# Strassen's seven products for every second weight chunk in the first three down halves of a two-block float32 kernel

## Chip, cores and metric

The kernel runs on one core of one Trainium2 chip. The metric is the device time of one execution in microseconds (us), lower is better. Times "before" are those of the kernel as it stood; the change is then made to it and nothing else.

## The reference

Two blocks work on 256 tokens of width 2048, all in float32. The first is a mixer (a gated linear recurrence beside a banded attention) followed by an MLP; the second is an attention block with 16 meta tokens. The change touches the MLP of the first block alone:

```python
u = rms_norm(h, norm_mlp_w[l])
h = h + jnp.square(jax.nn.relu(u @ w_up[l])) @ w_down[l]    # w_up 2048 x 8192, w_down 8192 x 2048
```

## The kernel before

**Weights as a stream of chunks.** Every weight matrix of the program goes through one ring. A chunk is 256 rows by 512 columns of a weight (two tiles of 128 rows, CK = 2, by CW = 512 columns, 512 KB), and eight chunks (NC) are a group: 2048 rows by 512 columns. The ring has four slots (SLOTS). For each chunk SyncE's queue issues one load into `raw` (`chunk`, line 366) as soon as the lower half of the chunk four places earlier is done (`wlo_ready`). Then the float32 values are split in two parts of which TensorE can multiply each in one pass: ScalarE copies `raw` to `whi` with rounding (`split_hi`, line 887), and it waits for the load and for TensorE being done with the chunk four places earlier (`pe_done`). VectorE subtracts, `wlo = raw - whi` (`split_lo`, line 1301). TensorE waits for `wlo_ready` of the chunk and multiplies three times for each product: high by high, high by low and low by high. ScalarE and VectorE work four chunks ahead of TensorE (LEAD = 4): in their loops, step `k` of a group splits chunk `k + 4`.

**The MLP** is cut into four quarters of 2048 hidden columns (`quarter`: line 682 for TensorE, 1100 for ScalarE, 1588 for VectorE, 1970 for GpSimd). A quarter has two halves of four groups each. In the up half `chunk_t` (line 430) makes four hidden blocks of 128 columns by 256 tokens for each group in PSUM: ScalarE takes the relu, GpSimd squares it (`relu2`), ScalarE copies the square to the high part in `ya_hi` or `yb_hi`, VectorE subtracts for the low part. These are the activations of the down half. There `chunk_n` (line 451) sets tokens stationary and streams weights: for each of two row tiles, two token tiles and two pieces of 256 columns it issues three matmuls, so 2 x 2 x 2 x 3 = 24 matmuls of 256 columns for each chunk. After a group VectorE adds the sum, times a factor for each token, to `h` (`scalar_tensor_tensor`, line 1617). Up and down groups take banks 0 to 3 of PSUM by turns (`set_free`).

**Order on the engines.** Each engine works its list in order. On VectorE and ScalarE the splits are the backbone, and the rest of a group stands behind the splits of the group. GpSimd has nothing but the squares in these quarters, 16 in all.

**The names that the change brings.** In a chunk, A is the 256 tokens by 256 rows of activations and B the 256 rows by 512 columns of weights. Cut in 2 by 2 blocks their product takes eight block products, each 128 tokens by 128 rows by 256 columns; Strassen's scheme (in Winograd's form) takes seven, with sums of blocks on both sides.

Of the kernel before, what the change touches and what calls it, by code (L numbers as in the profile page):

```python
# [60 lines left out]
C_END = C_OUT2 + 4 * NC  # L61

# [49 lines left out]
def program(nc, x, w_in, lb_logits, hg_norm_w, rel_bias, w_branch_a, w_branch_b, w_out, norm_mix_w,  # L112
# [3 lines left out]
    with ExitStack() as ctx:  # L116
# [100 lines left out]
        relu2 = at("relu2", 96, [P, 4, T])  # L217
        fin_w = at("fin_w", 80, [P, D])
# [66 lines left out]
        br_m, br_hi, br_ready = sem("br_m"), sem("br_hi"), sem("br_ready")  # L285
        up_sq, up_hi, up_ready = [sem(n) for n in ("up_sq", "up_hi", "up_ready")]
# [40 lines left out]
        def kv_banks(j):  # L327

            return (0, 4) if j % 2 == 0 else (2, 6)

# [96 lines left out]
        def _(pe):  # L427
# [23 lines left out]
            def chunk_n(c0, k, kt0, xh, xl, s, first, last, halves=range(NT), pieces=1):  # L451

                pe.wait_ge(wlo_ready, c0 + k + 1)
                for j in range(CK):
                    kt = kt0 + j
                    for t in halves:
                        toks = slice(t * P, (t + 1) * P)
                        for piece in range(pieces):
                            cols = slice(piece * CW // pieces, (piece + 1) * CW // pieces)
                            for i, (v, w) in enumerate(((xh, whi), (xh, wlo), (xl, whi))):  # L460
                                ins = mm(ps[:, 2 * s + t, cols], v[:, kt, toks], w[:, k % SLOTS, j, cols],  # L461
                                         start=first and j == 0 and i == 0 and piece == 0,
                                         stop=last and j == CK - 1 and i == 2, skip_group_check=True)
# [218 lines left out]
            def quarter(q, first=False, last=False):  # L682

                c0 = C_FF + 8 * NC * q
                for g in range(4):
                    pe.wait_ge(set_free[g % 2], G_IN // 2 + 6 + 4 * q + g // 2)
                    for k in range(NC):
# [4 lines left out]
                        chunk_t(c0 + NC * g, k, CK * k, x2hi, x2lo, blocks(g % 2), T, k == 0, k == NC - 1)  # L692
                for g in range(4):
                    pe.wait_ge(set_free[g % 2], G_IN // 2 + 8 + 4 * q + g // 2)
                    for k in range(NC):
                        pe.wait_ge(up_ready, 4 * q + k // 2 + 1)
                        uh, ul = (ya_hi, ya_lo) if k < NC // 2 else (yb_hi, yb_lo)
# [3 lines left out]
                        chunk_n(c0 + 4 * NC + NC * g, k, CK * (k % (NC // 2)), uh, ul, g % 2, k == 0, k == NC - 1,  # L701
# [182 lines left out]
        def _(act):  # L884
            f = nc.scalar.activation

            def split_hi(c0, k):
# [4 lines left out]
                f(whi[:, k % SLOTS], raw[:, k % SLOTS], ACT.Copy).then_inc(whi_ready, 1)  # L892

# [206 lines left out]
            def quarter(q, first=False, last=False):  # L1100
                c0 = C_FF + 8 * NC * q
                for g in range(4):
                    for k in range(NC):
                        split_hi(c0 + NC * g, LEAD + k)
# [8 lines left out]
                    f(relu[:], pset(g % 2), ACT.Relu).then_inc(set_free[g % 2], 1)  # L1113
# [3 lines left out]
                for g in range(4):  # L1117
                    for k in range(NC):
                        split_hi(c0 + 4 * NC + NC * g, LEAD + k)
                        if last and g >= 1:  # L1120
# [7 lines left out]
                            if k == 4:  # L1128
                                scaled_squares(g - 1)

# [160 lines left out]
        def _(dve):  # L1291
# [9 lines left out]
            def split_lo(c0, k):  # L1301

                dve.wait_ge(whi_ready, c0 + k + 1)
                tt(wlo[:, k % SLOTS], raw[:, k % SLOTS], whi[:, k % SLOTS], ALU.subtract).then_inc(wlo_ready, 1)  # L1304

# [282 lines left out]
            def quarter(q, first=False, last=False):  # L1588
                c0 = C_FF + 8 * NC * q
                for g in range(4):  # L1590
                    for k in range(NC):
                        split_lo(c0 + NC * g, LEAD + k)
# [14 lines left out]
                for g in range(4):  # L1607
                    for k in range(NC):
                        split_lo(c0 + 4 * NC + NC * g, LEAD + k)
                        if last and g >= 1 and k == 1:  # L1610
                            wide_lower(g - 1)
                        if last and g == 1 and k == 5:
                            nc.vector.tensor_copy(xw_lo[:, :, T:TM], mlo).then_inc(m_lo_placed, 1)
                    dve.wait_ge(pe_done, c0 + 4 * NC + NC * (g + 1))
# [249 lines left out]
        def _(pool):  # L1864
# [192 lines left out]
```

## Time and profile before

| | |
|---|---|
| time, median of 3 runs | 1884.91 us (1884.53 to 1887.14) |
| the profiled execution | 1885.47 us, of which the span from first to last instruction is 1883.7 us |
| TensorE busy | 1870.7 us (99%), 15001 matmuls recorded |
| VectorE, ScalarE busy | 1101.3 us (58%), 890.0 us (47%) |
| GpSimd busy | 149.8 us (8%), 133 instructions |
| granted TensorE clock, mean | 0.999 |
| HBM | 183 GB/s over the span |

The quarters of the MLP lie from about 725 to 1428 us of the span. "Busy" is the time in which an engine had an instruction under way; the durations of single matmuls overlap, so the pace of TensorE is read from a stretch of many of them and not from the mean of one. A line of the trace ends with the idle time of the engine just before the instruction and what ended it. L1304 is VectorE's split of the weights, L892 ScalarE's, L447 and L461 are the matmuls of `chunk_t` and `chunk_n`, and L371 the loads.

### The profile page before, as it was taken

Reading aid. Unit: us, or ns where it says so; the run is one execution under the profiler, and the core shown is the slowest. Engines: PE = TensorE matmul, PEld = TensorE weight load, DVE = VectorE, ACT = ScalarE, POOL = GpSimd, SP = SyncE. Lnnn points to the kernel's source line nnn. Section 1 sums busy time; section 2 is a strip of 40 time slices with the busy share of each in tenths; the row PEclk is TensorE's granted clock in tenths of the full one; section 3 lists DMA queues with packets and bytes.
Section 4 is the critical chain, followed back from the end, with each engine's and each line's share of the span. In section 5 each row is a group of like instructions: output and inputs, shape, how many; then the busy total and the mean of one; then the engine's idle time right before and its main releaser. Section 6 shows DMA issues by size and latency. Waiting matters only on the chain.

```text
span 1883.7 us, 37025 instructions
## 1 busy us (share of the span) xinstructions
PE 1870.7 (99%) x15001; PEld 1802.9 (96%) x15001; DVE 1101.3 (58%) x1270; ACT 890.0 (47%) x1171; POOL 149.8 (8%) x133
## 2 busy tenths in 40 slices
PE   9999999999999999999999999999999999999998
PEld 9989998999999989999999999999989999899998
DVE  6645766667655555545445545544566556867664
ACT  6544443465544445443444344334554345574543
POOL 1001322411001100000000000001010000000000
PEclk9999999999999999999999999999999999999999
DMA  8666566566665666666666666666656665355464
GB/s 270 191 178 176 182 179 179 163 197 180 177 223 192 214 186 185 185 203 195 196 192 194 197 188 197 197 192 193 193 184 179 177 175 159 113 168 146 157 191 145
DMA packets 176927, 347.94 MB, mean 185 GB/s; under 512 B 11152, under 2 KB 11360, under 8 KB 176256
## 3 DMA queue, kind: packets, MB, share of 16 engines
q1 hardware_dynamic: 174176, 337.76, 58.8%
q0 software_dynamic: 2608, 8.08, 1.7%
q8 instruction: 114, 1.87, 0.4%
q14 instruction: 29, 0.24, 0.0%
HBM read 342.37 MB, written 2.10 MB: 183 GB/s over the span
## 4 chain that ended last, share of the span: by engine, by line
PE 98%; DVE 1%; ACT 0%; DMA 0%; issue 0%; SPq 0%; DVEq 0%; ACTq 0%
PE ps L447 60%; PE ps L461 32%; PE ps L551 1%; PE ps L784 1%; PE ps L774 1%; PE ps L794 1%; PE ps L751 0%; PE ps L479 0%; PE ps L762 0%; PE ps L602 0%; PE ps L594 0%; PE ps L492 0%; DMA x_nat<-in_x_dram 0%; PE ps L613 0%; PE ps L735 0%; ACT whi L892 0%
## 5 line engine op out<-in xcount | busy, mean ns | idle before, releaser
L1304 DVE TENSOR_TENSOR wlo<-raw,whi 128x1024 fp32r<-128x1024 f32 x631 | 796.6, 1269 | 688.2 <-ACT whi L892 687.3
L892 ACT ACTIVATE whi<-raw 128x1024 fp32r<-128x1024 f32 x631 | 664.9, 1059 | 883.2 <-PE ps L447 549.8
L447 PE MATMUL ps<-xhi,whi 128*128 128x256 f32 (+1 forms) x1904 | 541.5, 284 | 0.3 <-DVE qrot L1667 0.3
L447 PE MATMUL ps<-xhi,wlo 128*128 128x256 f32 (+1 forms) x1904 | 531.3, 279 | 0.0
L447 PE MATMUL ps<-xlo,whi 128*128 128x256 f32 x1664 | 462.5, 278 | 0.0
L447 PEld LDWEIGHTS ps<-xhi,whi 128*128 128x128 f32 x1904 | 359.3, 189 | 8.8 <-issue 6.2
L447 PEld LDWEIGHTS ps<-xhi,wlo 128*128 128x128 f32 x1904 | 357.9, 188 | 0.0
L447 PEld LDWEIGHTS ps<-xlo,whi 128*128 128x128 f32 x1664 | 313.2, 188 | 1.2 <-issue 0.5
L447 PE MATMUL ps<-x2hi,whi 128*128 128x256 f32 x1024 | 282.8, 276 | 0.0
L447 PE MATMUL ps<-x2lo,whi 128*128 128x256 f32 x1024 | 282.7, 276 | 0.0
L447 PE MATMUL ps<-x2hi,wlo 128*128 128x256 f32 x1024 | 282.7, 276 | 0.0
L447 PEld LDWEIGHTS ps<-x2lo,whi 128*128 128x128 f32 x1024 | 192.2, 188 | 0.2
L447 PEld LDWEIGHTS ps<-x2hi,whi 128*128 128x128 f32 x1024 | 192.2, 188 | 0.2
L447 PEld LDWEIGHTS ps<-x2hi,wlo 128*128 128x128 f32 x1024 | 192.2, 188 | 0.0
L461 PE MATMUL ps<-whi,ya_hi 128*128 128x256 f32 (+1 forms) x464 | 133.8, 288 | 0.0
L461 PE MATMUL ps<-whi,ya_lo 128*128 128x256 f32 (+1 forms) x464 | 133.7, 288 | 0.0
L461 PE MATMUL ps<-wlo,ya_hi 128*128 128x256 f32 (+1 forms) x464 | 133.6, 288 | 0.0
L461 PE MATMUL ps<-whi,yb_lo 128*128 128x256 f32 (+1 forms) x452 | 131.8, 292 | 0.0
L461 PE MATMUL ps<-whi,yb_hi 128*128 128x256 f32 (+1 forms) x452 | 131.7, 291 | 0.0
L461 PE MATMUL ps<-wlo,yb_hi 128*128 128x256 f32 (+1 forms) x452 | 131.6, 291 | 0.0
L461 PE MATMUL ps<-whi,xlo 128*128 128x512 f32 x256 | 100.8, 394 | 0.0
L461 PE MATMUL ps<-whi,xhi 128*128 128x512 f32 x256 | 100.2, 391 | 0.0
(371 smaller groups left out, 2727.3 us busy)
## 6 DMA issues: line engine op xcount, KB each, us to landing
raw<-in_w_in_dram SPq DMA_DIRECT2D x279, 512.0 KB, 3.8
raw<-in_w_up_dram SPq DMA_DIRECT2D x128, 512.0 KB, 3.8
raw<-in_w_down_dram SPq DMA_DIRECT2D x128, 512.0 KB, 4.0
raw<-in_w_out_dram SPq DMA_DIRECT2D x64, 512.0 KB, 4.4
raw<-in_w_branch_a_dram SPq DMA_DIRECT2D x16, 512.0 KB, 5.2
raw<-in_w_branch_b_dram SPq DMA_DIRECT2D x16, 512.0 KB, 4.6
x_nat<-in_x_dram SPq DMA_DIRECT2D x4, 512.0 KB, 7.1
rel<-in_rel_turned_dram POOLq DMA_DIRECT2D x8, 256.0 KB, 4.4
```

The source lines that it names most:

```text
L447: ins = mm(outs[b], w[:, k % SLOTS, j, cols], v, start=start, stop=last and j == CK - 1 and i == 2, skip_group_check=True)
L461: ins = mm(ps[:, 2 * s + t, cols], v[:, kt, toks], w[:, k % SLOTS, j, cols], start=first and j == 0 and i == 0 and piece == 0, stop=last a ...
L551: ins = mm(misc[:, hd // 4, (hd % 4) * P:(hd % 4 + 1) * P], k_both[:, hd, :], spread(qp[:, hd, 0:1], *both_tiles), start=True, stop=True)
L774: ins = nc.tensor.transpose(ps[:, 6, i * P:(i + 1) * P], p[:, i * P:(i + 1) * P], ident[:])
L784: ins = mm(ps[:, 7, 0:P], pt2[:, u % 2, i * P:(i + 1) * P], v, start=i == 0, stop=i == 2)
L794: ins = mm(ps[:, 7, 0:T], v, pt_heads[hd % 2][:, i, :], start=i == 0, stop=i == 2)
L892: f(whi[:, k % SLOTS], raw[:, k % SLOTS], ACT.Copy).then_inc(whi_ready, 1)
L1304: tt(wlo[:, k % SLOTS], raw[:, k % SLOTS], whi[:, k % SLOTS], ALU.subtract).then_inc(wlo_ready, 1)
```

## The change

In quarters 0 to 2 (`SEVEN_Q = 3`), every even chunk of a down group is multiplied by `chunk_seven`; the odd chunks and the last quarter stay with `chunk_n`. That makes 3 quarters x 4 groups x 4 = 48 chunks with 7 x 3 = 21 matmuls in the place of 24.

- **TensorE**: seven products into partial sums of 256 columns, numbered 0 to 7, in four banks; the odd chunks add to partials 0 to 3, which are the output's own blocks. Up groups now use banks 4-5, 6-7, 0-1, 2-3, down groups by turns banks 4-7 and 0-3.
- **GpSimd**: for each such chunk `weight_sums`, one instruction of 128x512 and two of 128x256 in float32, each of which waits for the one before. For each up group, behind the square, `token_sums`: four instructions of 128x128. The three weight sums of down group 0, chunks 0, 2 and 4, stand ahead of the square of up group 3.
- **ScalarE and VectorE**: in such a chunk three quarters of `raw` are split as before (128x768), and then the four weight sums (128x1024, `t_hi` and `t_lo`). VectorE signals `wlo_ready` at the end of `t_lo`, and the slot is loaded anew only then. Token sums are split once for each up group (128x512).
- **The end of a down group**: ScalarE copies one partial to SBUF (`c_first`, 128x256), VectorE adds partials from PSUM to `c_sum` by four additions of 128x512, two of them in step 0, one and one more in step 1 of the next group (behind its splits), and step 2 adds `c_sum`, scaled, to `h` by two instructions of 128x512.

```diff
+SEVEN_Q = QUARTERS - 1
+SEVEN_EACH = NC // 2
+UP_SETS = (2, 3, 0, 1)
...
+            def chunk_seven(c0, k, b, first, last):
+                pe.wait_ge(wlo_ready, c0 + k + 1)
...
+                parts = ((0, sums(3), weights(1, 0)), (1, given(odd, 0), weights(1, 1)),
+                         (3, given(odd, 1), weight_sums(3)), (4, given(even, 0), weights(0, 1)),
+                         (5, sums(1), weight_sums(1)), (6, sums(2), weight_sums(2)), (7, sums(0), weight_sums(0)))
+                for n, (vh, vl), (wh, wl) in parts:
+                    for i, (v, w) in enumerate(((vh, wh), (vh, wl), (vl, wh))):
+                        ins = mm(ps[:, b + n // 2, (n % 2) * T:(n % 2) * T + T], v, w,
+                                 start=first and i == 0 and n in (0, 3, 4, 6), stop=last and i == 2,
+                                 skip_group_check=True)
+                ins.then_inc(pe_done, 1)
...
                         pe.wait_ge(up_ready, 4 * q + k // 2 + 1)
+                        if seven(q, k):
+                            pe.wait_ge(s_ready, 4 * q + k // 2 + 1)
+                            chunk_seven(c0 + 4 * NC + NC * g, k, down_banks(g), k == 0, k == NC - 2)
+                            continue
...
+            def split_hi_seven(c0, k, n):
+                act.wait_ge(raw_in[k % SLOTS], 4 * c0 + 16 * (k // SLOTS + 1))
+                act.wait_ge(pe_done, c0 + k - SLOTS + 1)
+                f(whi[:, k % SLOTS].rearrange("p j c -> p (j c)")[:, T:4 * T],
+                  raw[:, k % SLOTS].rearrange("p j c -> p (j c)")[:, T:4 * T], ACT.Copy).then_inc(whi_ready, 1)
+                act.wait_ge(t_summed, n + 1)
+                f(t_hi[:, k // 2 % 2], t_sum[:, k // 2 % 2], ACT.Copy).then_inc(t_upper, 1)
...
+                    if not last:
+                        act.wait_ge(pe_done, c0 + 4 * NC + NC * (g + 1))
+                        f(c_first[:], ps[:, down_banks(g) + 2, 0:T], ACT.Copy).then_inc(c_copied, 1)
...
+            def split_lo_seven(c0, k, n):
+                dve.wait_ge(whi_ready, c0 + k + 1)
+                part = [v[:, k % SLOTS].rearrange("p j c -> p (j c)")[:, T:4 * T] for v in (wlo, raw, whi)]
+                tt(*part, ALU.subtract)
+                dve.wait_ge(t_upper, n + 1)
+                tt(t_lo[:, k // 2 % 2], t_sum[:, k // 2 % 2], t_hi[:, k // 2 % 2], ALU.subtract).then_inc(wlo_ready, 1)
...
+            def seven_out(q, g, step):
+                b, n = down_banks(g), 16 * q + 4 * g
+                if step == 0:
+                    dve.wait_ge(pe_done, C_FF + 8 * NC * q + 4 * NC + NC * (g + 1))
+                    dve.wait_ge(c_copied, 4 * q + g + 1)
+                    tt(summed(1, 4), spread(c_first[:, 0:1], [0, 2], [1, T]), partial(b, 1, 6), ALU.add).then_inc(c_step, 1)
+                    dve.wait_ge(c_step, n + 1)
+                    tt(summed(5, 6), summed(4), partial(b, 5, 7), ALU.add).then_inc(c_step, 1)
...
+                        if g >= 1 and k < 3 and not last:
+                            seven_out(q, g - 1, k)
...
+            def weight_sums(q, g, k):
+                c0, n = C_FF + 8 * NC * q + 4 * NC + NC * g, seven_at(q, g, k)
+                w, to = raw[:, k % SLOTS], t_sum[:, k // 2 % 2]
+                pool.wait_ge(raw_in[k % SLOTS], 4 * c0 + 16 * (k // SLOTS + 1))
+                pool.wait_ge(wlo_ready, c0 + k - SLOTS + 1)
+                tt(to[:, 0:2, :], spread(w[:, 0, 0:1], [0, 2], [1, T]), spread(w[:, 0, T:T + 1], [T, 2], [1, T]),
+                   ALU.subtract).then_inc(t_step, 1)
+                pool.wait_ge(t_step, 2 * n + 1)
+                tt(to[:, 2, :], w[:, 1, 0:T], to[:, 0, :], ALU.subtract).then_inc(t_step, 1)
+                pool.wait_ge(t_step, 2 * n + 2)
+                tt(to[:, 3, :], w[:, 1, T:2 * T], to[:, 2, :], ALU.subtract).then_inc(t_summed, 1)
...
-            with pool.Fori(0, QUARTERS) as q:
+            with pool.Fori(0, SEVEN_Q) as q:
                 for g in range(4):
-                    pool.wait_ge(set_free[g % 2], G_IN // 2 + 6 + 4 * q + g // 2 + 1)
-                    tt(relu2[:], relu[:], relu[:], ALU.mult).then_inc(up_sq, 1)
+                    if g == 3:
+                        for k in range(0, 6, 2):
+                            weight_sums(q, 0, k)
+                    squared(q, g)
+                    token_sums(q, g)
+                for g in range(4):
+                    for k in range(0, NC, 2):
+                        if g > 0 or k == 6:
+                            weight_sums(q, g, k)
+            for g in range(4):
+                squared(SEVEN_Q, g)
```

## Rows read from the trace of the kernel before

**Rows 1.** The chain that ended last, from 725 us: start, us, what.

```profile
732.02 81.62 PE ps L447 x720
813.64 87.07 PE ps L461 x756
```

**Rows 2.** Busy time by engine in an up half and the down half behind it.

```profile
core 0: us, PE busy (x) PEld busy (x) DVE busy (x) ACT busy (x) POOL busy (x), PEclk, DMA share, GB/s
725.40:812.50 87.10, 87.10 (x770) 87.05 (x769) 44.52 (x43) 43.49 (x48) 6.12 (x3) 1.00 0.64 190
812.50:899.70 87.20, 87.20 (x764) 86.88 (x763) 44.38 (x40) 35.73 (x34) 2.02 (x1) 1.00 0.64 195
```

**Rows 3.** The same columns in the first 6 us.

```profile
0.00:6.00 6.00, 2.79 (x12) 2.38 (x12) 0.40 (x3) 1.49 (x2) 4.22 (x12) 1.00 0.50 155
```

**Rows 4.** Timeline from up group 3 to down group 0: start, us, instruction, idle before it.

```profile
813.74 1.06 ACT L892 ACTIVATE whi<-raw 128x1024 fp32r<-128x1024 f32 x1 [1.66 <-PE ps L447]
...
817.84 1.06 ACT L1116 ACTIVATE yb_hi<-relu 128x1024 fp32r<-128x1024 f32 x1 [2.13 <-POOL relu L1973]
...
815.79 2.02 POOL L1973 TENSOR_TENSOR relu<-relu 128x1024 f32<-128x1024 f32 x1 [19.74 <-ACT relu L1113]
...
814.83 1.23 DVE L1304 TENSOR_TENSOR wlo<-raw,whi 128x1024 fp32r<-128x1024 f32 x1 [1.50 <-ACT whi L892]
818.93 1.23 DVE L1606 TENSOR_TENSOR yb_lo<-relu,yb_hi 128x1024 fp32r<-128x1024 f32 x1 [2.88 <-ACT yb_hi L1116]
820.08 2.35 DVE L1304 TENSOR_TENSOR wlo<-raw,whi 128x1024 fp32r<-128x1024 f32 x2
```

**Rows 5.** GpSimd's groups by form: count, busy us, mean ns, idle before.

```profile
L1973 POOL TENSOR_TENSOR relu<-relu 128x1024 f32<-128x1024 f32 x16 | 32.4, 2025 | 663.3 <-ACT relu L1113 663.3
L1894 POOL TENSOR_TENSOR pairs<-pairs,masked 128x512 f32<-128x512 f32 x12 | 15.5, 1295 | 107.9 <-DVE masked L1463 107.9
L1967 POOL TENSOR_TENSOR both<-part_a,part_b 128x1024 f32<-128x1024 f32 x4 | 9.6, 2400 | 141.6 <-DVE part_b L1570 141.6
```

**Rows 6.** Timeline of VectorE and GpSimd where the last quarter scales h.

```profile
1387.18 2.42 POOL L1979 TENSOR_TENSOR h<-h,fin_w 128x1024 f32<-128x1024 f32 x1 [20.43 <-PE ps L479]
...
1387.35 3.33 DVE L1304 TENSOR_TENSOR wlo<-raw,whi 128x1024 fp32r<-128x1024 f32 x1 [1.52 <-ACT whi L892]
```

**Rows 7.** Timeline of both where the recurrence adds its tiles.

```profile
335.56 2.41 POOL L1899 TENSOR_TENSOR acc<-acc,masked 128x1024 f32<-128x1024 f32 x1 [21.97 <-DVE masked L1469]
340.27 3.31 POOL L1899 TENSOR_TENSOR acc<-acc,pairs 128x1024 f32<-128x1024 f32 x1 [2.30 <-DVE pairs L1469]
...
335.87 3.18 DVE L1304 TENSOR_TENSOR wlo<-raw,whi 128x1024 fp32r<-128x1024 f32 x1 [0.39 <-ACT whi L892]
338.97 1.21 DVE L1469 TENSOR_TENSOR pairs<-pairs,tri 128x1024 f32<-128x1024 f32 x1
340.11 5.69 DVE L1304 TENSOR_TENSOR wlo<-raw,whi 128x1024 fp32r<-128x1024 f32 x3
```

**Rows 8.** Timeline of both at one level of the recurrence.

```profile
238.06 1.29 POOL L1894 TENSOR_TENSOR pairs<-pairs,masked 128x512 f32<-128x512 f32 x1 [1.76 <-DVE masked L1463]
239.31 1.39 POOL L1912 TENSOR_TENSOR g_even<-g_odd 128x128 f32<-128x128 f32 x1
...
238.54 1.90 DVE L1304 TENSOR_TENSOR wlo<-raw,whi 128x1024 fp32r<-128x1024 f32 x1 [0.56 <-ACT whi L892]
```

**Rows 9.** VectorE's groups by form.

```profile
L1304 DVE TENSOR_TENSOR wlo<-raw,whi 128x1024 fp32r<-128x1024 f32 x631 | 796.6, 1269 | 688.2 <-ACT whi L892 687.3
L1617 DVE SCALAR_TENSOR_TENSOR h<-ps,rstd,h 128x512 f32<-128x512 f32 x32 | 22.4, 743 | 0.0
L1463 DVE TENSOR_TENSOR masked<-ps,masks 128x512 f32<-128x512 f32 x12 | 8.2, 680 | 0.0
L1493 DVE TENSOR_TENSOR o_hg<-o_hg,rs_hg 128x512 f32<-128x512 f32 x4 | 2.7, 684 | 0.0
```

**Rows 10.** Loads of the down weights: count, KB each, us from issue to landing.

```profile
raw<-in_w_down_dram SPq DMA_DIRECT2D x128, 512.0 KB, 4.0
```

More of the change, by code:

```diff
@@ L217, in program @@
         relu2 = at("relu2", 96, [P, 4, T])
+        s_sum = at("s_sum", 92, [P, 4, P])
+        t_sum = at("t_sum", 100, [P, 2, 4, T])
+        c_sum = at("c_sum", 108, [P, 8, T])
+        c_first = at("c_first", 94, [P, T])
+        s_hi, s_lo = [v[:, 0:4 * 4 * P].rearrange("p (g i t) -> p g i t", g=4, i=4) for v in x_flat]
+        t_hi, t_lo = [v[:, 4 * 4 * P:KT * T].rearrange("p (n i c) -> p n i c", n=2, i=4) for v in x_flat]
         fin_w = at("fin_w", 80, [P, D])
@@ L466, in chunk_n, with given, sums, weights @@
                 return ins
+            def chunk_seven(c0, k, b, first, last):
+                pe.wait_ge(wlo_ready, c0 + k + 1)
+                uh, ul = (ya_hi, ya_lo) if k < NC // 2 else (yb_hi, yb_lo)
+                even, odd = CK * k % (NC), CK * k % (NC) + 1
+                toks = slice(0, P), slice(P, T)
+                slot, turn = k % SLOTS, k // 2 % 2
+                def given(kt, t):
+                    return uh[:, kt, toks[t]], ul[:, kt, toks[t]]
+                def sums(i):
+                    return s_hi[:, k // 2, i, :], s_lo[:, k // 2, i, :]
+                def weights(j, half):
+                    cols = slice(half * T, half * T + T)
+                    return whi[:, slot, j, cols], wlo[:, slot, j, cols]
+                def weight_sums(i):
+                    return t_hi[:, turn, i, :], t_lo[:, turn, i, :]
+                parts = ((0, sums(3), weights(1, 0)), (1, given(odd, 0), weights(1, 1)),
[7 more added lines that the diff above has]
+                ins.then_inc(pe_done, 1)
             def blocks(s):
@@ L700, in quarter @@
                         whole = last and g >= 1 or g == 3 and k == NC - 1
[L701 removed]
+                        chunk_n(c0 + 4 * NC + NC * g, k, CK * (k % (NC // 2)), uh, ul,
+                                g % 2 if last else down_banks(g) // 2, k == 0, k == NC - 1,
                                 pieces=1 if whole else 2)
@@ L1613, in quarter @@
                             nc.vector.tensor_copy(xw_lo[:, :, T:TM], mlo).then_inc(m_lo_placed, 1)
+                    if not last:
+                        if g == 3:
+                            for step in range(3):
+                                seven_out(q, g, step)
+                        continue
                     dve.wait_ge(pe_done, c0 + 4 * NC + NC * (g + 1))
@@ new lines, in token_sums @@
+            def token_sums(q, g):
+                first, second = [[relu2[:, i, t * P:(t + 1) * P] for i in range(2)] for t in range(NT)]
+                pool.wait_ge(up_sq, 4 * q + g + 1)
+                tt(s_sum[:, 1, :], second[0], first[0], ALU.subtract).then_inc(s_step, 1)
+                tt(s_sum[:, 0, :], second[0], second[1], ALU.add)
+                pool.wait_ge(s_step, 2 * (4 * q + g) + 1)
+                tt(s_sum[:, 2, :], s_sum[:, 1, :], second[1], ALU.add).then_inc(s_step, 1)
+                pool.wait_ge(s_step, 2 * (4 * q + g) + 2)
+                tt(s_sum[:, 3, :], first[1], s_sum[:, 2, :], ALU.subtract).then_inc(s_summed, 1)
```

70 lines of the change are left out of this document (64 added, 6 removed).

## The prediction

> **What bounds the kernel now.** I read first the chain that ended last. In the MLP it is TensorE alone: an up half is one piece of `chunk_t` matmuls, the down half behind it one piece of `chunk_n` matmuls, 87.07 us for its 32 chunks [rows 1]. So a chunk takes 87.07 / 32 = 2.721 us and a matmul of 256 columns 2.721 / 24 = 0.1134 us. Next the busy times by stage: in a down half TensorE is busy for 87.2 of 87.2 us, VectorE for 44.4, ScalarE for 35.7, GpSimd for 2.0 [rows 2]. Last the timeline: a split comes when TensorE is done with the chunk four places before (ScalarE at 813.74, VectorE done at 816.06), while three chunks, 3 x 2.721 = 8.2 us, still lie ahead of TensorE. The lead is 8.2 - 2.3 = 5.8 us [rows 4]. The chip is bound by the count of matmuls, and anything that shortens the list pays, as long as VectorE keeps ahead.
>
> **What is removed.** 3 of 24 matmuls in 48 chunks: 16 x 3 x 0.1134 = 5.44 us for each down half, 16.3 us in all. An even chunk takes 2.381 us, a pair 5.10.
>
> **What is added on GpSimd.** The reader should look at what two engines do to each other. GpSimd scaled `h` from 1387.18 to 1389.60, and a split that VectorE began at 1387.35 took 3.33 us in the place of 1.23 [rows 4, 6]: it ended at 1390.68, which is 1389.45 + 1.23. So it stood still until 0.15 us short of GpSimd's end. The same at 335.87: 3.18 us, end 339.05 = 337.82 + 1.23, with GpSimd's end at 337.97 [rows 7]. At 340.27 it is the other way: VectorE was first (340.11), GpSimd's addition took 3.31 us and not 2.41, about the 1.0 us that VectorE's first split still had, and VectorE's other two then waited (three in 5.69 us, where two back to back take 2.35 [rows 4, 7]). And the 1.39 us of a GpSimd instruction of only 128x128 at 239.31 is mostly waiting for VectorE's split that ended at 240.44 [rows 8]. Two instructions that both read two tensors of SBUF take turns, whole ones.
>
> The three weight sums read two SBUF tensors each. 128x512 takes 1.30 us, 128x1024 2.40 [rows 5]; the line through both gives 0.74 us for 128x256 and 0.47 for 128x128. The other end for 128x256 is the 1.39 us of rows 8; I take 0.74, since the additions of rows 5 are the nearest in kind and the 1.39 is explained. Less the 0.14 us at the end in which VectorE already runs, a chunk's sums close the way for 1.16 + 0.60 + 0.60 = 2.36 us. [...]
>
> **What is added on VectorE.** For a pair of chunks: 128x768 of the even chunk, between 0.68 us for 128x512 and 1.22 for 128x1024 [rows 4, 9], so 0.95; the sums' lower half and the odd chunk 1.17 each, back to back [rows 4]. For a group's end: four additions of 128x512 from PSUM at 0.68 and two of 0.74 [rows 9], 4.2 us where 1.5 stood.
>
> **The sum for one quarter.** Take the 32 steps from the split of down chunk 0 (TensorE done with chunk 4 of up group 3) to that of the last down chunk. TensorE would want that last one after three up chunks and 31 down chunks: 3 x 2.721 + 16 x 2.381 + 15 x 2.721 = 87.1 us. In this stretch VectorE has 16 x 3.29 = 52.6, three group ends 12.6, the lower half of the last squares 1.2 and of the last token sums 0.7: 67.1 us. Alone it would fit. GpSimd closes the way for 15 x 2.36 = 35.4 (the first chunk's sums run before the stretch), for the square 1.9 and for four token sums 4 x 0.33 = 1.3: 38.6 us. Together 105.7. To this come 2 us in which VectorE waits for ScalarE (today it stands idle 2.88 us ahead of the last squares' lower half [rows 4]; most of that is now GpSimd's). From it goes what runs side by side: VectorE's additions from PSUM read one SBUF tensor, 3 x 2.7 = 8.2 us in the stretch; no row shows one under GpSimd, so between 0 and 8.2 could overlap, and I take half. 105.7 + 2 - 4.1 = 103.6 us, 16.5 more than TensorE wants; the lead of 5.8 us is already in the 87.1. Less 5.44 gained: +11.1 for each quarter, +33 us for three. The profiled execution would go from 1885.47 (span 1883.7) to 1918.7; the median of the runs before is 0.6 lower, so **1918 us**.
>
> The Trainium skill (SBUF — State Buffer, "two separate sides") calls the pair of ports that VectorE and GpSimd share an exclusive lock for a whole instruction, which only VectorE's instructions with two SBUF inputs (or in a two-port mode) ask for. By that rule all 8.2 us would overlap, and the sum would be 1906. The first half of it is what rows 6 and 7 show; the second no row here shows.
>
> **The rest costs nothing, as long as its cover is there.** ScalarE's copies grow from 1.06 us to at most 2 x 1.06 in an even chunk, 16 x 1.06 = 17 us on 35.7 of 87 [rows 2]. The copy `c_first` waits for TensorE's end of a group, but stands behind splits that are four chunks ahead. The loads keep their size, but a slot is free only after the sums' lower half; this matters in rival B. The weight sums for down chunk 4 stand ahead of the square of up group 3; they push that square back by some 2 us, and the squares are wanted only at chunk 6 of the down half, 16 us on. The banks are freed later by `c_sum`, and the next use is a group away. In the up halves VectorE has over 40 us idle [rows 2] for token sums.
>
> **Rivals.**
> A, **the gain comes whole: 1869 us** (1885.5 - 16.3, less 0.6). VectorE's 67.1 us fit in 87.1, if GpSimd's sums fall into its idle time. For: today the two hardly meet. Against: together they have 105.7 us for 87.1. It decides the other way if the turns cost under (87.1 + 5.4 - 67.1 - 2 + 4.1) / 38.6 = 71% of GpSimd's time; rows 6 and 7 show over 90%.
> B, **the round of a slot bounds, 1945 us.** From the end of an even chunk's split to that of the same slot's next: load 4.0 us [rows 10], sums 2.8, each of the three behind one of VectorE's instructions, up to 3 x 1.17, ScalarE's copy 1.06, VectorE's 1.23 behind 1.3 of the other slot's sums: 13.9 us for four chunks, 111 for 32, 24 over 87.1, so +19 net for each quarter, +57 to 60. With half of the waits it is 12 and lies under my 103.6. For: six places to wait in one row. Against: VectorE can't be first at every one.
> C, **TensorE's clock falls** in the waits that now cut up its work, from 2.4 to 1.2 GHz. Matmuls of the down halves would take up to twice as long, over 2000 us. Against: in the first 6 us of the program TensorE had matmuls under way for 2.79 us only and was granted 1.00 [rows 3]; the new waits are under 2 us each.
> D, the costs and the gain meet at about 1885: turns of some 71%.
>
> **How the numbers follow.** Forecast 0.61 (1900 to 1935: all of the PSUM additions under cover and no idle, 105.7 - 8.2 = 97.5, +15 us; none under cover and 4 us idle, 109.7, +51 at the far end); B 0.20; A 0.12; D 0.04; C 0.03. About 0.2% is what a measurement of this kernel tells from no change. Faster 0.12, same 0.03, slower 0.85. The range leaves out A, D, C and the far end of B: 1894 to 1955; the 1.39 us for 128x256 would add 32 x 0.65 = 21 us for each quarter and is left out too, since it is waiting that is counted already. Most cases have one sign, so one range is enough.
>
> **What would show it.** In the down halves of quarters 0 to 2: TensorE idle before the matmuls of `chunk_seven`, released by VectorE's `t_lo`; VectorE busy for more than 90% of such a half, with splits of 1.9 to 2.5 us wherever GpSimd runs; GpSimd about 55 to 60 us busy, its instructions of 128x256 at 0.74 us alone and near 2 behind VectorE; a half of some 98 us where 87.1 stood; 0.1134 us a matmul as before; up halves and the last quarter unchanged. Splits at 1.23 us beside a busy GpSimd would make the forecast wrong and A right; VectorE idle for a fifth of the half, ahead of `t_lo` and released by ScalarE, would make it B.

## Result: 2.0% slower, and the profile after

The changed kernel takes **1922.2 us** (median of 4, 1921.56 to 1924.0) against 1885.01, a ratio of 1.0196 with the 95% interval 1.0184 to 1.0208. The forecast was 1918, with a range of 1894 to 1955. The profiled execution took 1921.56 us. Its page, the span and the engines' busy times:

```profile
span 1919.8 us, 37397 instructions
PE 1875.8 (98%) x14857; PEld 1802.7 (94%) x14857; DVE 1249.7 (65%) x1378; ACT 931.4 (49%) x1243; POOL 391.6 (20%) x325
```

TensorE has fewer matmuls and is busy for longer than before: its matmuls ran slower (experiment 1). VectorE is up by 148 us and GpSimd by 242. The stages of quarter 0, a down half and the up half behind it, with the columns of [rows 2]:

```profile
core 0: us, PE busy (x) PEld busy (x) DVE busy (x) ACT busy (x) POOL busy (x), PEclk, DMA share, GB/s
813.15:912.90 99.75, 87.97 (x710) 85.42 (x709) 86.01 (x68) 46.99 (x53) 65.97 (x47) 1.00 0.53 165
913.00:1000.00 87.00, 87.00 (x769) 87.00 (x768) 50.37 (x46) 41.49 (x43) 21.55 (x21) 1.00 0.61 196
```

The down half takes 99.75 us where 87.07 stood [rows 1], the up half is unchanged. VectorE is busy for 86 of the 99.75 us and not for 44. The span is 36.1 us longer, 12.0 for each down half. TensorE's waits for the sums and for the plain chunks behind them, over the whole program (us in all, times, the longest):

```profile
PE ps L528 <- DVE xlo L1410: 24.1, 18, 3.3
PE ps L495 <- DVE wlo L1402: 5.2, 6, 1.8
```

So it waits for the lower half of the sums, as the prediction said (`t_hi` and `t_lo` lie in the buffers xhi and xlo and are named so; L1410 writes `t_lo`). The groups of GpSimd's sums over the program and of VectorE's splits in the down half show the price of each (count, busy us, mean ns, then idle before):

```profile
L2143 POOL TENSOR_TENSOR t_sum<-raw 128x512 f32<-128x512 f32 x48 | 78.1, 1627 | 83.8 <-DMA raw<-in_w_down_dram 83.8
L2146 POOL TENSOR_TENSOR t_sum<-raw,t_sum 128x256 f32<-128x256 f32 x48 | 73.1, 1523 | 3.8
L2148 POOL TENSOR_TENSOR t_sum<-raw,t_sum 128x256 f32<-128x256 f32 x48 | 60.1, 1251 | 3.8
```

```profile
L1402 DVE TENSOR_TENSOR wlo<-raw,whi 128x1024 fp32r<-128x1024 f32 x16 | 27.2, 1707 | 0.0
L1410 DVE TENSOR_TENSOR xlo<-t_sum,xhi 128x1024 fp32r<-128x1024 f32 x15 | 24.7, 1644 | 8.8 <-ACT xhi L971 8.8
L1408 DVE TENSOR_TENSOR wlo<-raw,whi 128x768 fp32r<-128x768 f32 x15 | 19.5, 1299 | 0.0
L1435 DVE SCALAR_TENSOR_TENSOR h<-c_sum,rstd,h 128x512 f32<-128x512 f32 x6 | 6.1, 1062 | 0.0
```

A 128x256 instruction of GpSimd, 0.74 us alone, takes 1.25 to 1.52 in the mean; a 128x768 part of a split 1.30 where 0.95 was assumed, a full split 1.71 where 1.23 stood [rows 4], an addition to `h` 1.06 for 0.74 [rows 9]. They take turns, and the timeline shows single ones, GpSimd's lines and VectorE's:

```profile
850.00 1.59 POOL L2146 TENSOR_TENSOR t_sum<-raw,t_sum 128x256 f32<-128x256 f32 x1
851.67 0.74 POOL L2148 TENSOR_TENSOR t_sum<-raw,t_sum 128x256 f32<-128x256 f32 x1
...
850.92 0.67 DVE L1423 TENSOR_TENSOR c_sum<-c_first,ps 128x512 f32<-128x512 f32 x1
...
862.36 2.18 POOL L2143 TENSOR_TENSOR t_sum<-raw 128x512 f32<-128x512 f32 x1 [2.69 <-DMA raw<-in_w_down_dram]
864.62 1.61 POOL L2146 TENSOR_TENSOR t_sum<-raw,t_sum 128x256 f32<-128x256 f32 x1
...
862.15 1.21 DVE L1410 TENSOR_TENSOR xlo<-t_sum,xhi 128x1024 fp32r<-128x1024 f32 x1
863.28 2.33 DVE L1402 TENSOR_TENSOR wlo<-raw,whi 128x1024 fp32r<-128x1024 f32 x1
```

GpSimd's 128x512 was issued at 862.36 and waited for VectorE's `t_lo`, which ended at 863.36; then VectorE's next split waited for it. Another thing to see is at 850.92: VectorE's addition from PSUM ran in 0.67 us beside GpSimd's instruction that ended at 851.59. It had to wait for nothing. The same holds for all 48 of these additions, whose four groups have means of 677 to 688 ns, where [rows 9] have 680 (one of the groups):

```profile
L1423 DVE TENSOR_TENSOR c_sum<-c_first,ps 128x512 f32<-128x512 f32 x12 | 8.1, 677 | 0.0
```

That is the point that no row of the kernel before showed, and here the trace agrees with the rule of the Trainium skill (SBUF — State Buffer, "two separate sides"): an instruction with one SBUF input doesn't ask for the shared ports.

At the head of the down half there is a second kind of delay. GpSimd makes the sums of chunk 4 ahead of the square of up group 3:

```profile
814.99 1.49 POOL L2143 TENSOR_TENSOR t_sum<-raw 128x512 f32<-128x512 f32 x1 [2.05 <-DMA raw<-in_w_down_dram]
...
818.95 1.90 POOL L2124 TENSOR_TENSOR relu<-relu 128x1024 f32<-128x1024 f32 x1
...
820.88 1.06 ACT L1205 ACTIVATE yb_hi<-relu 128x1024 fp32r<-128x1024 f32 x1 [4.98 <-POOL relu L2124]
...
824.37 2.30 DVE L1410 TENSOR_TENSOR xlo<-t_sum,xhi 128x1024 fp32r<-128x1024 f32 x1
```

ScalarE stood idle for 4.98 us ahead of the copy of the square and not for 2.13 [rows 4], and the splits of chunk 4 stand behind that copy in its list. The lower half of that chunk's sums was done at 826.68, and TensorE had waited 2.9 us for it; in quarters 1 and 2 it waited 3.3 and 2.8 us at the same place. These three are 9.0 of the 29.3 us of waits above.

Last the chain that ended last, for one round of a slot (start, us, what; short pieces left out):

```profile
826.99 3.83 DMA raw<-in_w_down_dram
...
830.98 1.50 POOL t_sum L2143
...
832.57 1.07 POOL t_sum L2146
...
833.71 1.62 POOL t_sum L2148
...
835.35 1.07 ACT xhi L971
...
836.44 2.33 DVE xlo L1410
...
839.06 3.91 DMA raw<-in_w_down_dram
```

From load to load it is 12.07 us for four chunks for which TensorE wants 10.2: the load 3.9, GpSimd's three instructions 4.2 (2.8 alone), ScalarE's copy 1.07, VectorE's `t_lo` 2.33 (1.23 alone). This was one of the shorter rounds. From the second `t_lo` of a slot on, the 36 rounds of slots 0 and 2 in the three halves took 10.9 to 14.6 us from the end of one `t_lo` to that of the next, 12.5 in the mean. The down half of quarter 0 is then made up so: 13.7 us up to TensorE's start of chunk 4, the wait at the head included, six rounds of slot 0, 75.3 us, and 10.9 us for the last four chunks. The chain isn't the slot's round alone: from 848.8 to 863.4 it runs through VectorE's list, with the four additions to `c_sum`, the two to `h` and the splits between them.

### The profile page after: what moved, and what is told of

Read it like the earlier page. It is cut to its first block, busy times and chain, and to the rows that moved or that the text cites. A ratio compares the mean times of both kernels' runs of the same rounds, so it can differ in the third digit from the quotient of the medians.

```text
span 1919.8 us, 37397 instructions
## 1 busy us (share of the span) xinstructions
PE 1875.8 (98%) x14857; PEld 1802.7 (94%) x14857; DVE 1249.7 (65%) x1378; ACT 931.4 (49%) x1243; POOL 391.6 (20%) x325
## 4 chain that ended last, share of the span: by engine, by line
PE 57%; issue 24%; POOL 7%; DMA 5%; DVE 5%; ACT 2%; SPq 0%; POOLq 0%; DVEq 0%; ACTq 0%
PE ps L481 37%; PE ps L495 14%; DMA raw<-in_w_down_dram 5%; POOL t_sum L2143 2%; DVE xlo L1410 2%; POOL t_sum L2146 2%; POOL t_sum L2148 1%; POOL relu L2124 1%; ACT xhi L971 1%; DVE wlo L1402 1%; PE ps L616 1%; PE ps L854 1%; PE ps L844 1%; PE ps L864 1%; PE ps L821 0%
## 5 line engine op out<-in xcount | busy, mean ns | idle before, releaser
L1402 DVE TENSOR_TENSOR wlo<-raw,whi 128x1024 fp32r<-128x1024 f32 x583 | 764.0, 1318 | 535.9 <-ACT whi L962 535.2
L962 ACT ACTIVATE whi<-raw 128x1024 fp32r<-128x1024 f32 x583 | 613.2, 1058 | 720.2 <-PE ps L481 518.1
L971 ACT ACTIVATE xhi<-t_sum 128x1024 fp32r<-128x1024 f32 x48 | 50.9, 1060 | 136.5 <-POOL t_sum L2148 136.5
L2124 POOL TENSOR_TENSOR relu<-relu 128x1024 f32<-128x1024 f32 x16 | 32.0, 2001 | 364.7 <-ACT relu L1202 364.7
L495 PE MATMUL ps<-wlo,xhi 128*128 128x512 f32 x256 | 100.1, 391 | 0.0
L1410 DVE TENSOR_TENSOR xlo<-t_sum,xhi 128x1024 fp32r<-128x1024 f32 x48 | 76.4, 1592 | 30.2 <-ACT xhi L971 30.2
L2143 POOL TENSOR_TENSOR t_sum<-raw 128x512 f32<-128x512 f32 x48 | 78.1, 1627 | 83.8 <-DMA raw<-in_w_down_dram 83.8
L481 PE MATMUL ps<-xw_lo,whi 128*128 128x272 f32 x320 | 91.7, 287 | 0.0
```

Of the source, the lines that this page charges most:

```text
L481: ins = mm(outs[b], w[:, k % SLOTS, j, cols], v, start=start, stop=last and j == CK - 1 and i == 2, skip_group_check=True)
L971: f(t_hi[:, k // 2 % 2], t_sum[:, k // 2 % 2], ACT.Copy).then_inc(t_upper, 1)
L1410: tt(t_lo[:, k // 2 % 2], t_sum[:, k // 2 % 2], t_hi[:, k // 2 % 2], ALU.subtract).then_inc(wlo_ready, 1)
L2143: tt(to[:, 0:2, :], spread(w[:, 0, 0:1], [0, 2], [1, T]), spread(w[:, 0, T:T + 1], [T, 2], [1, T]), ALU.subtract).then_inc(t_step, 1)
```

## Experiments

Twelve kernels ran. In the table a down half is the mean of the three in the profiled execution, from TensorE's first matmul in one to its first in the up half behind; before it is 87.1 us. The profiled execution isn't always near the median: with chunks 0 and 4 it was the fastest of four (1892.4), with the shift of 832 bytes it took 1880.9.

| kernel | time, us | ratio (95%) | down half |
|---|---|---|---|
| as changed | 1922.2 | 1.0196 (1.0184 to 1.0208) | 99.3 |
| no weight sums | 1880.3 | 0.9972 (0.9963 to 0.9982) | 85.4 |
| early load | 1905.7 | 1.0102 (1.0086 to 1.0119) | 93.5 |
| chunks 0 and 6 | 1887.7 | 1.0011 (1.0001 to 1.0020) | 87.9 |
| chunks 0 and 4 | 1895.8 | 1.0053 (1.0037 to 1.0070) | 89.9 |
| sums on VectorE | 1902.7 | 1.0085 (1.0069 to 1.0102) | 92.7 |
| own tiles, full sums | 1920.8 | 1.0181 (1.0162 to 1.0200) | 99.2 |
| own tiles, half sums | 1892.0 | 1.0035 (1.0023 to 1.0048) | 88.4 |
| own tiles, no sums | 1868.9 (one run) | | 81.6 |
| plain matmuls, no sums | 1887.0 (one run) | | 87.1 |
| two banks, no sums | 1882.0 (one run) | | 85.4 |
| 0 and 6, sums shifted by 64 bytes | 1886.2 | 1.0007 (0.9998 to 1.0016) | 85.9 |
| 0 and 6, weight sums shifted by 832 bytes | 1884.0 | 0.9994 (0.9981 to 1.0007) | 85.3 |

**1. No weight sums.**

```diff
-                tt(to[:, 0:2, :], spread(w[:, 0, 0:1], [0, 2], [1, T]), spread(w[:, 0, T:T + 1], [T, 2], [1, T]),
-                   ALU.subtract).then_inc(t_step, 1)
-                pool.wait_ge(t_step, 2 * n + 1)
-                tt(to[:, 2, :], w[:, 1, 0:T], to[:, 0, :], ALU.subtract).then_inc(t_step, 1)
-                pool.wait_ge(t_step, 2 * n + 2)
-                tt(to[:, 3, :], w[:, 1, T:2 * T], to[:, 2, :], ALU.subtract).then_inc(t_summed, 1)
+                tt(to[:, 0, 0:2], w[:, 0, 0:2], w[:, 0, 2:4], ALU.subtract).then_inc(t_summed, 1)
```

Besides, GpSimd sets `t_sum` to 1 once in each quarter.

> The changed kernel without its weight sums: for each even chunk GpSimd subtracts two elements and signals, the rest stays (ScalarE and VectorE split the sums' tile, TensorE makes 21 matmuls). Left out: the three GpSimd instructions of a chunk, so the sums' values are constants. Forecast's theory (GpSimd's sums close VectorE's way): VectorE has 67 us for 87 and the whole gain comes, 1869 us, down halves of some 82 us. Slot-round theory: a round is 4.5 + 0.3 + 1.06 + 1.23 = 7.1 us, also 1869. Theory that the new matmuls, their banks or the group ends cost: well over 1880.

1880.3 us: 42 of the changed kernel's microseconds hang on GpSimd's sums, and TensorE waits for nothing in the down halves. But 11 us of the gain are missing, and there is no idle time in which they could lie. They are in the matmuls themselves. First matmuls of three chunks in a row, plain, seven products, plain (start, us; of the lines between two chunks none is shown):

```profile
831.74 0.28 PE L495 MATMUL ps<-whi,yb_hi 128*128 128x256 f32 x1
...
834.57 0.28 PE L528 MATMUL ps<-whi,xhi 128*128 128x256 f32 x1
...
837.08 0.28 PE L495 MATMUL ps<-whi,ya_hi 128*128 128x256 f32 x1
```

The plain chunk takes 834.57 - 831.74 = 2.83 us for 24, 117.9 ns a matmul, the other 2.51 us for 21, 119.5 ns, where every chunk ran at 113.3 before. 48 x (2.51 - 2.38) + 48 x (2.83 - 2.72) = 11.5 us.

**2. Early load.** The load waits for the readers of `raw`, not for `t_lo`:

```diff
+                if read is not None:
+                    sp.wait_ge(t_summed, read + 1)
+                    sp.wait_ge(part_read, read + 1)
...
-                tt(*part, ALU.subtract)
+                tt(*part, ALU.subtract).then_inc(part_read, 1)
```

> The load into the slot of an even chunk waits for VectorE's part of the split and GpSimd's sums and no longer for the lower half of the sums. Nothing is left out, the work on each engine is the same. Forecast's theory (turns of whole instructions, the sum of both engines' time bounds): that sum stays, at least 97.5 us for a stretch for which 103.6 was forecast, so 1900 to 1922 us. Slot-round theory (rival B): a round loses the sums' upper and lower half, 1.06 + 1.2 to 2.3 us, and the load is no longer behind them, so the down halves go to 83 to 88 us and the time to 1872 to 1888.

1905.7: 16.5 us less than the changed kernel, without any change to what the engines compute. So the slot's round did bound, and rival B had hold of something; but the time is far from B's 1872 to 1888 and within the 1900 to 1922 of the forecast's theory. The rounds are 11.6 us in the mean. That the turns bound what is left is a reading and not shown by a run of its own; for it speaks that VectorE is busy for 86.6 and GpSimd for 70.7 of 94 us. The wait at the head (2.2 and 2.9 us in quarters 0 and 1) is still there. The columns are those of [rows 2]:

```profile
813.00:907.00 94.00, 89.59 (x725) 87.86 (x724) 86.61 (x68) 47.04 (x53) 70.70 (x49) 0.98 0.54 172
```

**3 and 4. Two chunks of eight.** `SEVEN_KS` is (0, 6) or (0, 4) and takes the place of "every even k".

```diff
-            return not (isinstance(q, int) and q >= SEVEN_Q) and k % 2 == 0
+            return not (isinstance(q, int) and q >= SEVEN_Q) and k in SEVEN_KS
```

> Only chunks 0 and 6 of a group by seven products, 24 chunks in all, 24 x 0.340 = 8.2 us less on TensorE. They use slots 0 and 2, each once in eight chunks. Forecast's theory: VectorE 59.5 us and GpSimd 19.7 us, 79 for a stretch in which TensorE wants 89.8: both fit, 1877 us. Slot-round theory: a round has eight chunks, 21 us, it fits too: 1877. A cost for each seven-product chunk (or each group end) on TensorE's own path: 1885 or more.

> Only chunks 0 and 4 of a group by seven products: the same work as with chunks 0 and 6, but both are in slot 0, which they use in every round of four chunks. Forecast's theory: the same sums as for chunks 0 and 6, 1877 us. Slot-round theory: a round of slot 0 takes 4.5 (load) + 2.8 (sums) + 2 to 3.5 (turns) + 1.06 + 1.23 = 11.6 to 13 us where TensorE wants 10.54 for four chunks, so down halves some 6 to 15 us longer than those of chunks 0 and 6: 1890 to 1920 us.

With chunks 0 and 6 TensorE waits for nothing in the down halves, and the time still misses 1877, by 24 x 0.13 + 72 x 0.11 = 11 us of slower matmuls: even the plain chunks between the others run at 117.9 ns.

Chunks 0 and 4 take 8 us more, and the forecast's sum of both engines' time, equal for both, doesn't see it. But the two kernels differ in more than the slots: with chunks 0 and 4 the sums of chunk 4 stand ahead of the square of up group 3, as in the changed kernel, and with 0 and 6 those of chunk 0 alone. ScalarE stands idle ahead of the copy of the square for 5.06 us with chunks 0 and 4 and for 2.13 with 0 and 6, and of the 4.8 us for which TensorE waits in the down halves with chunks 0 and 4, 2.9 are at that place (1.0, 0.9 and 0.9). Behind it a round of slot 0 takes 11.1 us in the mean, and TensorE at its slower pace wants 2.51 + 8.48 = 10.99 for four chunks. So here the round bounds by a hair, and a half is 2.0 us longer, not 6 to 15: the pair of runs doesn't decide for the round, as it was meant to.

**5. The sums on VectorE.**

```diff
             def split_lo_seven(c0, k, n):
+                w, to = raw[:, k % SLOTS], t_sum[:, k // 2 % 2]
+                dve.wait_ge(raw_in[k % SLOTS], 4 * c0 + 16 * (k // SLOTS + 1))
+                tt(to[:, 0:2, :], spread(w[:, 0, 0:1], [0, 2], [1, T]), spread(w[:, 0, T:T + 1], [T, 2], [1, T]),
+                   ALU.subtract).then_inc(t_step, 1)
...
```

> The weight sums move from GpSimd to VectorE, ahead of its part of the split (three additions more for each even chunk, 0.68 + 0.41 + 0.41 us); GpSimd keeps the squares and the token sums. Nothing is left out. Turns of whole instructions (forecast): VectorE has 16 x (3.3 + 1.5) + 12.6 + 1.9 = 91 us and GpSimd 3 in the stretch of 87.1, so some 4 to 7 us late each quarter instead of 16, 1890 us; with the slower matmuls that the run without sums showed (117.9 and 119.5 ns instead of 113.3) TensorE wants 91 us itself and VectorE is about even: 1880 to 1888. If GpSimd's instructions cost nothing by turns, moving them to the busier engine makes it slower than 1922.

1902.7: moving all the sums to the engine that is already the busier one saves 19.5 us: so much more does it cost to have them on GpSimd, with the turns, the places in the round and the square that stands behind them, than the additions themselves. At the head ScalarE is idle for 2.13 us again, and TensorE waits 0.3. But the time is over the 1880 to 1888 expected. VectorE's steps for one pair of chunks:

```profile
860.76 0.69 DVE L1408 TENSOR_TENSOR t_sum<-raw 128x512 f32<-128x512 f32 x1
861.48 0.43 DVE L1411 TENSOR_TENSOR t_sum<-raw,t_sum 128x256 f32<-128x256 f32 x1
861.94 0.42 DVE L1413 TENSOR_TENSOR t_sum<-raw,t_sum 128x256 f32<-128x256 f32 x1
862.28 0.95 DVE L1416 TENSOR_TENSOR wlo<-raw,whi 128x768 fp32r<-128x768 f32 x1
863.49 1.23 DVE L1418 TENSOR_TENSOR xlo<-t_sum,xhi 128x1024 fp32r<-128x1024 f32 x1 [0.26 <-ACT xhi L971]
864.63 1.22 DVE L1402 TENSOR_TENSOR wlo<-raw,whi 128x1024 fp32r<-128x1024 f32 x1
```

From 860.76 to 865.77 a pair is 5.01 us and not the 4.79 expected, for the waits between the dependent additions (0.03 to 0.04) and the one for ScalarE (0.26). With 4.2 for a group's end that makes 4 x 5.01 + 4.2 = 24.2 us a group, over TensorE's 21.4 at its slower pace. With 5.01 the expectation's own count is 16 x 5.01 + 12.6 + 1.9 + 3 = 97.7 us for the stretch and, less 5.44, 92.2 for the half; 92.7 was measured. VectorE's own list bounds here.

**6 to 8. What slows the matmuls.** All three start from the run without weight sums. First the even chunks by `chunk_n`; then two banks; then the tiles:

```diff
-                            chunk_seven(c0 + 4 * NC + NC * g, k, down_banks(g), k == 0, k == NC - 2)
-                            continue
```

```diff
-                        ins = mm(ps[:, b + n // 2, (n % 2) * T:(n % 2) * T + T], v, w,
-                                 start=first and i == 0 and n in (0, 3, 4, 6), stop=last and i == 2,
+                        ins = mm(ps[:, b + n // 2 % 2, (n % 2) * T:(n % 2) * T + T], v, w,
+                                 start=first and i == 0 and n in (0, 3), stop=last and i == 2,
```

```diff
-                    return s_hi[:, k // 2, i, :], s_lo[:, k // 2, i, :]
+                    return given(even + i % 2, i // 2)
...
-                    return t_hi[:, turn, i, :], t_lo[:, turn, i, :]
+                    return weights(i % 2, 1)
```

> From the run without weight sums, with the even chunks multiplied as before by 24 matmuls from whi and wlo (left out: the seven products; ScalarE, VectorE, GpSimd, the banks and the group ends are those of the changed kernel, so the sums are split and not used). Theory that something beside TensorE slows its matmuls (more work on other engines, waits): 117.9 ns a matmul, down halves of 90.5 us, 1895 us. Theory that the seven-product chunks themselves do it and the plain ones after them inherit it: 113.3 ns, down halves of 87.1 us, 1885 us.

> From the run without weight sums, the seven products go to two PSUM banks and not four, and only two matmuls of a group have the start flag (left out: partials 4 to 7 as sums of their own, they are added into 0 to 3). Theory that four open banks or four start flags slow the matmuls: 113.3 ns a matmul again, down halves of 81.6 us, 1869 us. Otherwise 117.9 and 119.5 ns and 1880 us as without the edit.

> From the run without weight sums, all seven products read whi, wlo and the activations' own tiles and none the sums' tiles (left out: the sums, by other blocks in their place); banks and count as in the changed kernel. Theory that reading the sums' tiles, or the values in them, slows the matmuls and those behind them: 113.3 ns, down halves of 81.6 us, 1869 us. Otherwise 117.9 and 119.5 ns and 1880 us.

Plain matmuls beside all the other work run at 113.3 ns, so that work doesn't slow them. The banks change nothing. Without the sums' tiles as operands, and without any wait of TensorE, the slow pace is gone, in the plain chunks too (plain, then seven products):

```profile
815.94 0.28 PE L495 MATMUL ps<-whi,ya_hi 128*128 128x256 f32 x1
...
818.66 0.28 PE L528 MATMUL ps<-whi,ya_hi 128*128 128x256 f32 x1
...
821.04 0.28 PE L495 MATMUL ps<-whi,ya_hi 128*128 128x256 f32 x1
```

2.72 us for 24 and 2.38 for 21, and 1868.9 us in all: the 1869 of rival A, the whole gain, once neither the sums nor their tiles stand in the way.

**9 and 10. The same tiles at other addresses**, in the kernel with chunks 0 and 6 (`S_AT`, `T_AT` are 16, 1040 and then 16, 1232):

```diff
-        s_hi, s_lo = [v[:, 0:4 * 4 * P].rearrange("p (g i t) -> p g i t", g=4, i=4) for v in x_flat]
-        t_hi, t_lo = [v[:, 4 * 4 * P:KT * T].rearrange("p (n i c) -> p n i c", n=2, i=4) for v in x_flat]
+        s_hi, s_lo = [v[:, S_AT:S_AT + 2 * 4 * P].rearrange("p (g i t) -> p g i t", g=2, i=4) for v in x_flat]
+        t_hi, t_lo = [v[:, T_AT:T_AT + 2 * 4 * T].rearrange("p (n i c) -> p n i c", n=2, i=4) for v in x_flat]
```

> The kernel with chunks 0 and 6 by seven products; the token sums are made for up groups 0 and 3 alone, since no others are read, and the split sums lie 64 bytes further on in their buffer (token sums at float 16, weight sums at float 1040). Nothing is left out. Theory that where the sums' tiles lie, relative to the other operand's address, slows the matmuls: the tiles now have the offset of the activations' tiles within 1 KB, matmuls may be back at 113.3 ns, down halves of 84.3 us and 1877 us. Theory that the values or anything else about the sums does it: 117.9 and 119.5 ns, 1887 us as without the shift.

> As the kernel shifted by 64 bytes, but the weight sums begin at float 1232, so that they have the offset of the weights' tiles whi within 1 KB, and the token sums that of the activations' tiles: each pair of operands then stands to each other as whi and ya_hi do, which run at 113.3 ns. Address theory: 113.3 ns, down halves of 84.3 us, 1877 us, and if only one of the two shifts does it, this one. Theory of values: 117.9 and 119.5 ns, 1887 us.

Half an answer. With 64 bytes, the plain chunks behind the first seven-product chunk of quarter 0 run at 113.3 ns, and from the next such chunk on at 117.7. Then the whole up half of quarter 1, with no sums' tile among its operands, runs at 117.8 as well, and from the second down half on plain chunks are at 113.3 again (the chain, from that up half on; 120 matmuls are five plain chunks):

```profile
901.59 90.45 PE ps L488 x768
...
994.50 13.60 PE ps L502 x120
...
1077.13 87.07 PE ps L488 x768
```

With 832 bytes the plain chunks of all three down halves run at 113.3 ns, the seven-product ones at 117 to 118. The place of the tiles matters, then, but neither place cures it, and the twelve runs of the second kernel scatter from 1879.1 to 1891.9 where the kernel before has 1884.0 to 1887.1. Its median is 1.8 us below the kernel before, and the interval doesn't exclude none: no version that computes the whole result beat it for certain.

**11 and 12. Own tiles with GpSimd's sums**, in full and at half the width:

```diff
-                tt(to[:, 0:2, :], spread(w[:, 0, 0:1], [0, 2], [1, T]), spread(w[:, 0, T:T + 1], [T, 2], [1, T]),
-                   ALU.subtract).then_inc(t_step, 1)
+                tt(to[:, 0, :], w[:, 0, 0:T], w[:, 0, T:2 * T], ALU.subtract).then_inc(t_step, 1)
...
-                tt(to[:, 2, :], w[:, 1, 0:T], to[:, 0, :], ALU.subtract).then_inc(t_step, 1)
+                tt(to[:, 2, 0:P], w[:, 1, 0:P], to[:, 0, 0:P], ALU.subtract).then_inc(t_step, 1)
...
-                tt(to[:, 3, :], w[:, 1, T:2 * T], to[:, 2, :], ALU.subtract).then_inc(t_summed, 1)
+                tt(to[:, 3, 0:P], w[:, 1, T:T + P], to[:, 2, 0:P], ALU.subtract).then_inc(t_summed, 1)
```

> The changed kernel with all its GpSimd, ScalarE and VectorE work, but the seven products read whi, wlo and the activations' own tiles (left out: the sums' values in the products). Matmuls should run at 113.3 ns. If the slower matmuls of the changed kernel were hidden behind its waits, the time stays within 3 us of 1922; if they come on top of the waits, it is 11 us lower, 1911. With 113.3 ns this is the case that the forecast priced: 1918.

> The same with GpSimd's three instructions of a chunk at half their width (128x256, 128x128, 128x128; left out besides: half of the sums), 1.7 us alone in the place of 2.8; their count and all waits stay. Turns by whole instructions, sum of both engines' time bounds (forecast): 16 x 1.1 = 17.6 us less in each down half, which is the whole delay, so TensorE bounds: 1869 to 1875. Round of a slot bounds: eight rounds each 1.1 to 1.5 us shorter, 9 to 12 us less for each half: 1885 to 1893. If only the number of turns counted: no change from the full width.

In full it takes 1920.8, within 3 us of 1922. But the matmuls did not run at 113.3 ns, as the expectation had it. In each down half they did so up to the wait at the head, and behind it they went on at 117.8, though no sums' tile is read (plain, seven products, plain: 2.83 and 2.47 us):

```profile
898.25 0.28 PE L495 MATMUL ps<-whi,ya_hi 128*128 128x256 f32 x1
...
901.08 0.28 PE L528 MATMUL ps<-whi,yb_hi 128*128 128x256 f32 x1
...
903.55 0.28 PE L495 MATMUL ps<-whi,yb_hi 128*128 128x256 f32 x1
```

In quarter 2 they were back at 113.3 from 1242.9 to 1254.5 us, between two more waits. So a wait of TensorE can bring on the slow pace as the sums' tiles can, and end it. The run shows that reading other tiles gains the changed kernel next to nothing; what the slow pace costs it was not measured. That its waits hide it is an argument: a round takes 12.5 us, and TensorE at the slow pace wants 10.7.

At half the width it is 28.8 us faster, 1892.0, and TensorE's waits shrink to 7.3 us:

```profile
PE ps L528 <- DVE xlo L1410: 5.8, 9, 1.1
PE ps L495 <- DVE wlo L1402: 1.5, 6, 0.7
```

The forecast's sum, 17.6 us less for each half, would have given 1869 to 1875; the round of a slot gave 1885 to 1893. By the trace a half is 10.8 us shorter: the rounds are 11.2 us in the mean and not 12.5, which is the 1.1 to 1.5 expected, and the waits at the head are 0.1 to 1.1 us and not 3.2 to 3.5. Here too the matmuls ran at 117.8 ns for most of each half, which the 1869 to 1875 hadn't; with it TensorE alone would want 16 x 2.47 + 16 x 2.83 = 84.8 us a half, still under the 88.4 measured.

## Why the prediction was right, point by point

- **What bounds now, and the gain.** Right. The 16.3 us are there: with the sums and their tiles away the kernel takes 1868.9, against 1869 worked out.
- **Turns of whole instructions.** Right, in both directions, and the sizes of GpSimd's instructions too: 0.74 us for 128x256 alone (at 851.67 above). VectorE's splits grew to 1.3 to 1.7 us in the mean, not everywhere to the 1.9 to 2.5 named.
- **The sum of both engines' time.** Its size was too high, and it wasn't the bound. "I take half" of VectorE's additions from PSUM failed: the 48 of them kept their 0.68 us in the mean. With all 8.2 us under cover the stretch is 99.5 and the half 94.0, and 93.5 is what the early load measured. The sentence on the rule of the Trainium skill (SBUF — State Buffer, "two separate sides") had that sum, 1906. The early load took 1905.7, but its matmuls ran slower and its clock fell for a while, which the sum hasn't, so the agreement is in part luck.
- **Rival B, dismissed under my 103.6.** This was the step that failed. "With half of the waits it is 12" (its terms give 11.5) is less than what a round measured, 12.5 us in the mean. The early load shows that the round bounds: the same work with the load out of it is 5.7 us a half shorter. The half-width sums agree, the kernels with two chunks of eight leave it open. It wasn't B alone: VectorE was idle for 13.7 us of the half, 8.8 of them ahead of `t_lo` and released by ScalarE, where B's sign was a fifth of the half. The two errors, a sum too high and a round put aside, met at nearly the same number; that 1918 lies so near 1922 is luck.
- **"The squares are wanted only at chunk 6."** Wrong. TensorE wants them there, but ScalarE copies them in its list ahead of the splits of chunk 4. The square began at 818.95, 3.1 us after the end of the relu that it reads, where some 2 were expected, and TensorE waited 9.0 us in all for chunk 4 at the heads. In total the sum covered it, as GpSimd's time. A kernel with the square ahead of the sums of chunk 4 was not run.
- **"0.1134 us a matmul as before".** Wrong: 117.9 and 119.5 ns, 11.5 us over the program as soon as TensorE bounds. Without it and without waits rival A would be 1869; with it, 1880.
- **Rival C, the clock.** Put aside because the new waits would be under 2 us. The longest is 3.3, and in quarters 1 and 2 the granted clock did fall, in quarter 2 behind a wait of 1.8 us. Around the wait at the head of the down half of quarter 1, with the columns of [rows 2]:

```profile
1010.00:1015.00 5.00, 1.65 (x12) 1.48 (x11) 5.00 (x4) 2.68 (x4) 4.84 (x4) 0.82 0.00 0
1015.00:1020.00 5.00, 5.00 (x25) 5.00 (x25) 4.69 (x4) 3.37 (x4) 2.85 (x3) 0.50 0.61 206
1020.00:1025.00 5.00, 5.00 (x44) 5.00 (x44) 4.69 (x5) 2.09 (x3) 3.79 (x3) 0.99 0.62 183
```

  TensorE had matmuls under way for 1.65 of 5 us, and in the next stretch was granted 0.50, which is 1.2 GHz, and gave 25 matmuls where 44 followed at the full level. It happened twice in this execution, and with the early load too (0.98 in its window above). What it costs wasn't measured alone; it lasted some 10 us of the span, in halves that wait anyway. The run at half the width, whose longest wait is 1.1 us, had none of it.
- **Busy shares.** Forecast: VectorE over 90%, GpSimd 55 to 60 us. Measured 86% and 66 us, which fits a round with some idle time in it more than a full VectorE.

## What to carry to other kernels

An instruction that reads two tensors of SBUF on GpSimd isn't free beside such a one on VectorE: count both engines' time as one budget, and leave out VectorE's instructions that read PSUM. Then follow one buffer round its ring, load, helper engines with their turns, split, release: that round can bound before any engine is full, and releasing the buffer at its last reader (here 16.5 us) is cheap. Look also at what stands behind a delayed instruction in each engine's list, not only at who reads its result. And after a change measure the pace of the matmuls themselves, since a saving of an eighth in the count of every second chunk was largely given back by 4 to 5.5% in the pace of all.

## What the runs showed that was not expected

Matmuls of 256 columns, weights loaded for each, have two paces here, 113.3 and 117.8 ns, for the same instructions on the same tiles, with TensorE idle nowhere and its clock granted in full. Two things brought on the slow one. One is operands in the sums' tiles, which themselves take 119.5: without weight sums the change began at the third product of the first such chunk, the first that streams a sums' tile, and the plain matmuls behind, whose operands had not moved, stayed at 117.9. The other is a wait of TensorE, in the kernels with own tiles. As a rule the pace came back at the next up half, but once, with the shift of 64 bytes, a whole up half ran at the slow one. It occurs far from the change too. From 60 to 100 us, where TensorE's work is that of the kernel before, the kernel before made 360 matmuls and the one with half sums 347 (columns of [rows 2]):

```profile
60.00:100.00 40.00, 40.00 (x360) 39.85 (x359) 23.47 (x26) 17.34 (x18) 0.00 (x0) 1.00 0.68 208
60.00:100.00 40.00, 40.00 (x347) 39.84 (x347) 22.94 (x25) 17.49 (x18) 0.00 (x0) 1.00 0.64 198
```

Where the tiles lie has a part in it (shifts by 64 and 832 bytes each changed which chunks were slow). The values of the weight sums have none that shows: with 1 in their place a chunk takes the same 2.51 and 2.83 us as with the true sums of chunks 0 and 6. What the slow pace is, and what carries it from one instruction to the next, was not settled.
